# Attention of a two-block model, stepped by single heads or by pairs of heads, on one Trainium2 core

## Chip, core and metric

The program runs on one NeuronCore of a Trainium2 chip. The metric is the device time of one execution in microseconds (us), smaller is better. PE is the matrix engine (TensorE), with PEld its weight loads; DVE is the vector engine, ACT the scalar engine, POOL GpSimd, SP the queue that starts the weight transfers. PSUM is the memory that PE writes, in banks of 128 partitions by 512 float32.

## The reference

Two blocks of a latent/context model, all in float32, with 256 latent and 256 context tokens of width 1024. The first block (gated linear attention, a state-space mixer, their feed-forward parts) and the feed-forward parts and experts of the second are not touched. The two attention mixers of the second block are. The even one has 8 heads of width 64: for latent queries a neighbourhood attention with a table of biases over 256 latent keys, joined in one softmax with 256 context keys; for context queries plain attention over the context. The odd one has, for latent queries only, 8 window heads with a sink, and 4 differential heads.

```python
def joint_softmax(parts, extra=None):
    m = parts[0].max(-1, keepdims=True)
    ...
    return [e / den for e in es]

def neighbourhood_attention(q, k, v, k_ctx, v_ctx, rpb):
    ...
    s_loc = jnp.einsum('bhrqd,bhrjkd->bhrqjk', qg, kg, preferred_element_type=jnp.float32) * scale + bias
    s_ctx = jnp.einsum('bhrqd,bhld->bhrql', qg, k_ctx, preferred_element_type=jnp.float32) * scale
    p_loc, p_ctx = joint_softmax([s_loc.reshape(b, h, rows, GRID_W, kh * GRID_W), s_ctx])
    ...

def diff_attend(q, kvs, lam):
    ...
        a = (p[:, :, 0] - lam * p[:, :, 1]).astype(v.dtype)
        o = jnp.einsum('bhqk,bhkd->bhqd', a, v)
```

## The kernel before

The program is a list of stages (lines 3198 to 3226). Each stage gives a part to PE, ACT and DVE, and the engines meet at a barrier between most stages. Products are numbered in the order in which PE makes them; a product takes the next of eight PSUM banks, PE waits in `B.empty` until that bank's earlier product was freed, and the reader waits in `B.full`.

The stage `Attention` (lines 2439 to 2608) runs twice: once with the items of `even_attention` (32 items: 4 feature tiles f by 4 query tiles t by 2 heads; t 0 and 1 are latent, with 512 keys and a bias, t 2 and 3 context, with 256 keys), once with those of `odd_attention` (16 window items with bias and sink, then 8 differential items of two score maps each). An item is one head and 128 queries. No queue or planner is in play: `for n in range(-ahead, N + 1)` steps through the items, with `ahead` = 2.

- **Scores** (`pair_pe`, L2480 to L2487; L2505 for the differential items). The items of a pair lie in the two halves of the partitions. For a biased pair PE first writes the bias into the bank as a product with the identity matrix (L2480), adds the scores of the 256 latent keys (L2483), then makes those of the context keys (L2487).
- **Maximum** on DVE (L2569), scaled and negated (L2574, or L2571 with the sink); then the **exponential** with its row sum on ACT (L2549). A differential item's two maps are weighed and combined on DVE (L2580 to L2583), in the same step in which their maxima are taken: DVE waits there for ACT.
- **Turned copies**: PE turns the weights 128 by 128 (L2512), ACT copies them to SBUF (L2539).
- **Outputs** (L2519): the turned weights are the stationary side, the values (64 or 128 columns) move. DVE divides by the row sum as it takes them out of PSUM (L2598); for differential items ACT first forms a root (L2556 to L2559).
- **Outputs turned**: every 8 even items (and every pair of query tiles in the odd stage) PE turns the outputs into feature-major order (L2528), and DVE copies them out (L2604, L2606).

```python
                    for it, bank in zip(its, banks):
                        pe.matmul(bank[:, 0:LAT], ident, it["bias"], start=True, stop=False)
```

Of the kernel before, what the change touches and what calls it, by code (L numbers as in the profile page):

```python
# [16 lines left out]
ALU = mybir.AluOpType  # L17
ACT = mybir.ActivationFunctionType
AX = mybir.AxisListType
# [220 lines left out]
def build(nc, I, out, stop=None):  # L240
    ctx = ExitStack()
    with ctx:
# [2053 lines left out]
        m_s = [[uT[:, 2 * i + j, :] for j in range(2)] for i in range(2)]  # L2296
        m_pt = [uT[:, 4 + i, :] for i in range(2)]
# [141 lines left out]
        class Attention(Stage):  # L2439
            all_banks = True  # L2440

            def __init__(self, items, turns, ahead):
                self.items, self.turns, self.ahead = items, turns, ahead
                self.maps = list(itertools.accumulate(len(it["maps"]) for it in items))
                N, order = len(items), []  # L2450
                for n in range(-ahead, N + 2):
                    for m in self.scored(n + ahead):
                        order += [("s", m, j) for j in range(len(items[m]["maps"]))]
                    if 0 <= n < N:
                        order += [("t", n, 0)]
                    if 0 <= n - 1 < N:
                        order += [("o", n - 1, 0)]
                    if n - 2 in turns:
                        order += [("f", n - 2, 0)]
# [3 lines left out]
            def paired(self, n):  # L2463
                first = n - n % 2
                return all(len(it["maps"]) == 1 for it in self.items[first:first + 2])

            def scored(self, n):

                if n >= len(self.items):
                    return []  # L2470
                return [n] if not self.paired(n) else [] if n % 2 else [n, n + 1]

            def pair_pe(self, pe, B, n):

                its = self.items[n:n + 2]
                banks = [B.empty(pe, self.order["s", n + a, 0]) for a in range(2)]
                nk, biased = its[0]["nk"], its[0]["bias"] is not None
                if biased:
                    for it, bank in zip(its, banks):
                        pe.matmul(bank[:, 0:LAT], ident, it["bias"], start=True, stop=False)  # L2480
                    for it, bank in zip(its, banks):
                        q, k = it["maps"][0]
                        pe.matmul(bank[:, 0:LAT], q, k[:, 0:LAT], start=False, stop=True)  # L2483
                at = LAT if biased else 0
                for it, bank in zip(its, banks):
                    q, k = it["maps"][0]
                    pe.matmul(bank[:, at:nk], q, k[:, at:nk], start=True, stop=True).then_inc(B.full_sem, 1)  # L2487

            def score(self, n, j):
                return m_s[n % 2][j][:, 0:self.items[n]["nk"]]  # L2490

            def stats(self, n, j):
                o = 12 * (n % 4) + 6 * j
                return [small[:, o + x:o + x + 1] for x in range(6)]

            def pe(self, pe, B):
                for (kind, n, j), i in self.order.items():
                    it = self.items[n]
                    nk = it["nk"]
                    if kind == "s" and self.paired(n):  # L2500
                        if n % 2 == 0:
                            self.pair_pe(pe, B, n)
# [19 lines left out]
                    else:  # L2522
                        dst, src, gain, made = self.turns[n]
                        for m in made:
                            B.freed(pe, self.order["o", m, 0])
# [839 lines left out]
```

## Time and profile before

| | us |
|---|---|
| median of 3 runs | 2741.61 (2740.02 to 2743.09) |
| the profiled execution | 2740.08 |
| its span, first to last instruction | 2738.2 |
| mean granted TensorE clock | 0.986 of 2.4 GHz |
| even attention stage, first product to last instruction | 1591.66 to 1651.74 |
| odd attention stage | 2238.36 to 2317.17 |

The profile counts an engine as busy while an instruction of its runs. A float32 matmul is two records ("x4" in the chain of waits is two matmuls), a transpose one record. Records of one group overlap, so their mean duration is no pitch; the pieces of the chain give the pitch.

### The profile page before, as it was taken

The page shows a single profiled execution, that of the slowest core. Times are in us where ns is not written, and L with a number is a line of the kernel's source. Part 1 is how long each engine was busy: PE and PEld are TensorE (multiplying, and loading weights), DVE is VectorE, ACT ScalarE, POOL GpSimd, SP SyncE. Part 2 cuts the span into 40 slices and gives each one's busy share as a digit, 9 for nine tenths or more (in the row PEclk, how much of TensorE's full clock was granted, in tenths as well). Part 3 has the DMA queues.
Part 4 walks back from the last instruction along what each step waited for, and adds up shares of the span by engine and source line. Part 5 has one row for each costly group of instructions (what it writes and reads, how often), then busy time and mean ns, then how long its engine had stood idle before and what let it go on. Part 6 is the DMA issues. An engine that isn't in the chain of part 4 may idle for free.

```text
span 2738.2 us, 38420 instructions
## 1 busy us (share of the span) xinstructions
PE 2635.7 (96%) x15510; PEld 1856.4 (68%) x15510; DVE 1402.4 (51%) x2724; ACT 571.8 (21%) x1142; POOL 546.1 (20%) x420
## 2 busy tenths in 40 slices
PE   8999999999989999999999999999999998999998
PEld 4348478888855665789964464888888756655554
DVE  2756376467757778533557542765555335410111
ACT  1216121100043333222022041100000325201110
POOL 0000035444400000047830000444453000000000
PEclk9999999999999999999999999999999998999998
DMA  9540035565242432545445301454543300499995
GB/s 349 196 163 32 31 136 195 176 207 178 88 108 74 112 98 80 162 158 166 154 130 202 137 32 46 170 191 162 163 141 118 119 1 1 166 419 411 415 410 228
DMA packets 222417, 446.71 MB, mean 163 GB/s; under 512 B 18873, under 2 KB 124152, under 8 KB 219162
## 3 DMA queue, kind: packets, MB, share of 16 engines
q1 hardware_dynamic: 180896, 329.78, 33.6%
q10 hardware_dynamic: 41338, 114.40, 12.5%
q8 instruction: 126, 2.06, 0.3%
q14 instruction: 57, 0.47, 0.0%
HBM read 443.01 MB, written 1.13 MB: 162 GB/s over the span
## 4 chain that ended last, share of the span: by engine, by line
PE 91%; DVE 5%; ACT 2%; issue 1%; POOL 0%; DVEq 0%; DMA 0%; ACTq 0%; SPq 0%; POOLq 0%
PE bank L1138 34%; PE bank L966 24%; PE bank L3010 5%; PE bank L990 4%; PE bank L3029 3%; PE bank L982 2%; PE bank_pair L3010 2%; PE bank L559 1%; PE bank L2519 1%; PE bank L3046 1%; PE bank L2095 1%; PE bank_pair L3029 1%; PE bank L2088 1%; PE bank L2512 1%; PE bank L2983 1%
## 5 line engine op out<-in xcount | busy, mean ns | idle before, releaser
L1138 PE MATMUL bank<-arena,slot 128*128 128x256 f32 (+1 forms) x3704 | 677.0, 343 | 6.3 <-DVE arena L1118 2.9
L1138 PEld LDWEIGHTS bank<-arena,slot 128*128 128x128 f32 x3704 | 605.0, 191 | 70.5 <-issue 8.0
L1151 POOL TENSOR_TENSOR slot<-slot 128x512 f32<-128x512 f32 (+3 forms) x208 | 269.8, 1297 | 1566.8 <-PE bank L1138 703.0
L966 PE MATMUL bank<-uT,slot 128*128 128x512 f32 (+2 forms) x1312 | 485.0, 525 | 2.7 <-ACT arena L2128 2.7
L966 PEld LDWEIGHTS bank<-uT,slot 128*128 128x128 f32 (+1 forms) x1312 | 246.7, 190 | 217.0 <-issue 204.8
L1138 PE MATMUL bank<-uT,slot 128*128 128x256 f32 (+1 forms) x1728 | 334.3, 350 | 8.6 <-ACT uT L731 8.4
L1138 PEld LDWEIGHTS bank<-uT,slot 128*128 128x128 f32 x1728 | 290.2, 191 | 46.3 <-ACT uT L731 12.1
L1152 POOL TENSOR_TENSOR slot<-slot 128x512 f32<-128x512 f32 (+3 forms) x208 | 287.2, 1381 | 0.0
L966 PE MATMUL bank<-arena,slot 128*128 128x256 f32 (+1 forms) x576 | 185.0, 484 | 3.8 <-DVE arena L1817 2.3
L966 PEld LDWEIGHTS bank<-arena,slot 128*128 128x128 f32 x576 | 111.9, 195 | 75.6 <-issue 66.7
L700 DVE SCALAR_TENSOR_TENSOR arena<-arena 128x1024 f32<-128x1024 f32 x95 | 122.3, 1297 | 18.8 <-issue 15.0
L990 PE MATMUL bank<-slot,uT 128*128 128x512 f32 (+1 forms) x320 | 120.1, 530 | 0.0
L990 PEld LDWEIGHTS bank<-slot,uT 128*128 128x128 f32 x320 | 55.8, 190 | 61.0 <-issue 60.6
L700 DVE SCALAR_TENSOR_TENSOR arena<-arena,bank_pair 128x1024 f32<-128x1024 f32 x78 | 94.7, 1215 | 2.3 <-issue 1.9
L2210 DVE SCALAR_TENSOR_TENSOR arena<-arena,vectors 128x512 f32<-128x512 f32 (+1 forms) x128 | 87.7, 685 | 4.6
L3010 PE MATMUL bank<-slot,arena 128*32 128x352 f32 x984 | 77.5, 459 | 0.0
L3144 DVE TENSOR_TENSOR arena<-bank_pair,arena 128x352 f32<-128x352 f32 x5 | 2.6, 514 | 140.8 <-PE bank_pair L3010 140.8
L1040 DVE SCALAR_TENSOR_TENSOR hT<-bank,mod,hT 128x256 f32<-128x256 f32 (+1 forms) x48 | 18.9, 435 | 104.1 <-PE bank L966 104.1
L1288 ACT ACTIVATE arena<-arena 128x2048 f32<-128x2048 f32 (+1 forms) x16 | 23.7, 1484 | 230.7 <-DVE arena L1193 173.0
L3144 DVE TENSOR_TENSOR arena<-bank,arena 128x352 f32<-128x352 f32 x16 | 7.9, 495 | 120.2 <-PE bank L3010 120.1
L982 PE MATMUL bank<-uT,slot 128*128 128x512 f32 (+1 forms) x192 | 65.9, 504 | 1.3 <-DVE uT L736 1.3
L3010 PE MATMUL bank<-arena 128*32 128x352 f32 x800 | 63.5, 459 | 0.0
(462 smaller groups left out, 3075.1 us busy)
## 6 DMA issues: line engine op xcount, KB each, us to landing
slot<-in_ffn_w SPq DMA_DIRECT2D x42, 2048.0 KB, 8.8
arena<-in_ada_wt ACTq DMA_DIRECT2D x100, 512.0 KB, 3.6
slot<-in_moe_w SPq DMA_DIRECT2D x62, 704.0 KB, 16.8
arena<-in_moe_w SPq DMA_DIRECT2D x52, 704.0 KB, 17.6
rstd<-in_ada_wt ACTq DMA_DIRECT2D x48, 512.0 KB, 3.5
slot<-in_moe_w SPq DMA_DIRECT2D x11, 2048.0 KB, 18.7
slot<-in_ssd_w_in SPq DMA_DIRECT2D x32, 512.0 KB, 6.9
uT<-in_ada_wt ACTq DMA_DIRECT2D x28, 512.0 KB, 3.6
```

The lines of the kernel that those rows point to most:

```text
L559: ins = pe.matmul(bank[:, :], first_w[:, k, n * P:n * P + P], uT[:, k, :], start=(k == 0), stop=(k == KD - 1))
L700: ins = dve.scalar_tensor_tensor(out=self.room[n % ROOMS] if last else self.spare, in0=self.room[n % ROOMS], scalar=1.0, in1=self.row(blk, ...
L966: ins = pe.matmul(bank[0:m, 0:t1 - t0], w[:, k, c0:c0 + m], x[:, k, t0:t1], start=(k == 0), stop=(k == kt - 1))
L982: ins = pe.matmul(bank[0:m, 0:t], w[:, k, c0:c0 + m], uT[:, k, 0:t], start=(k == 0), stop=(k == KD - 1))
L990: ins = pe.matmul(bank[:, 0:c1 - c0], x[:, k, t * P:t * P + P], w[:, k, c0:c1], start=(k == 0), stop=(k == kt - 1))
L1138: ins = pe.matmul(bank[:, u * n:u * n + n], a[:, k, u * P:u * P + P], x[:, k, :], start=(k == 0), stop=(k == self.h - 1))
L1151: pool.tensor_tensor(out[:, :, 0:c], x[:, :, 0:c], y[:, :, 0:c], op)
L1152: pool.tensor_tensor(out[:, :, c:2 * c], x[:, :, c:2 * c], y[:, :, c:2 * c], op)\
L2088: pe.matmul(o, s_xdt[k % 2][:, h, :], s_m[k % 2][:, h, :], start=True, stop=False)
L2210: ins = dve.scalar_tensor_tensor(out=acc, in0=s_raw[:, j, 0:n, tap:tap + LAT], scalar=vc("conv_w", 32 * tap + f), in1=acc, op0=ALU.mult, o ...
L3010: ins = pe.matmul(bank[32 * g:32 * g + 32, 0:FG], x, w[:, 0, c:c + FG], start=(k == 0), stop=(k == KD - 1))
L3029: ins = pe.matmul(banks[s][32 * c:32 * c + 32, 0:DG], m_turned_hid[:, q, s, :], w[:, q - a, c * DG:c * DG + DG], start=(q == 0), stop=(q = ...
```

## The change

The unit of both attention stages is now a pair: two heads of 128 queries each, or the two maps of a differential head (16 units per stage). In step j PE makes the scores of unit j + 2, turns the weights of unit j, makes the outputs of unit j - 1, and turns outputs of unit j - 3 (differential only).

- The bias product on PE is gone. DVE takes the maximum of the context keys, then one `tensor_tensor_reduce` adds the bias to the latent scores in PSUM and carries the maximum on. Scores are one matmul of up to 512 columns per head.
- The weights are divided by their row sum on DVE before they are turned (`normalise`), a step ahead; the differential combination (`combine`) also moved to the step after its exponentials.
- Outputs are made feature-major: the values are stationary (64 columns), the turned weights move (128 columns), and the two heads go to partitions 0 to 63 and 64 to 127 of one bank. DVE copies 128x128 to the result. The turning of outputs is left for differential heads alone.
- ACT's order in a step is: turned copies of j, root of j - 2, exponentials of j + 2, with one drain per pair where there was one per map.

```diff
-                if biased:
-                    for it, bank in zip(its, banks):
-                        pe.matmul(bank[:, 0:LAT], ident, it["bias"], start=True, stop=False)
-                    ...
+            def scores(self, pe, B, u):
+                it = self.units[u]
+                banks = [B.empty(pe, self.order["s", u, a]) for a in range(2)]
+                for (q, k), bank in zip(it["maps"], banks):
+                    pe.matmul(bank[:, 0:it["nk"]], q, k, start=True, stop=True).then_inc(B.full_sem, 1)
+
+            def turn(self, pe, B, u, a):
+                pe.wait_ge(*S("pn").taken("pe"))
+                bank = B.empty(pe, self.order["t", u, a])
+                for t in range(self.units[u]["nk"] // P):
+                    ins = pe.transpose(bank[:, t * P:t * P + P], self.score(u, a)[:, t * P:t * P + P], ident)
+                ins.then_inc(B.full_sem, 1)
+
+            def outputs(self, pe, B, u):
+                ...
+                        for a, v in enumerate(it["v"]):
+                            ins = pe.matmul(bank[64 * a:64 * a + 64, 0:P], v[t], self.weights(u, a, t), start=(t == 0),
+                                            stop=(t == last))
+                ins.then_inc(B.full_sem, 1)
-                for n in range(-self.ahead, N + 1):
-                    ...
+            def act(self, act, B, ch):
+                for j in self.steps():
+                    if self.has(j):
+                        self.copy_turned(act, B, j)
+                    if self.has(j - 2) and self.units[j - 2]["sub"]:
+                        self.output_root(act, B, ch, j - 2)
+                    if self.has(j + 2):
+                        self.exponentials(act, B, j + 2)
+
+            def maxima(self, dve, ch, B, u):
+                it, (mx, nm) = self.units[u], self.stats(u)[0:2]
+                for a in range(2):
+                    bank, m = B.full(dve, self.order["s", u, a]), mx[:, a:a + 1]
+                    at = 0 if it["bias"] is None else LAT
+                    n = ch(dve.tensor_reduce(m, bank[:, at:it["nk"]], AX.X, ALU.max))
+                    if at:
+                        ch.wait(n)
+                        s = bank[:, 0:at]
+                        n = ch(dve.tensor_tensor_reduce(out=s, in0=s, in1=it["bias"][a], scale=1.0, scalar=m, op0=ALU.add,
+                                                        op1=ALU.max, accum_out=m))
+                ch.wait(n)
+                ...
+
+            def normalise(self, dve, ch, u):
+                it, (den, es, rc) = self.units[u], self.stats(u)[2:5]
+                dve.wait_ge(*S("pr").taken("dve"))
+                ...
+                dve_link(ch, dve.reciprocal(rc, den))
+                for a in range(2):
+                    s = self.score(u, a)
+                    dve.tensor_scalar(s, s, rc[:, a:a + 1], None, ALU.mult).then_inc(*S("pn").given())
+
+            def dve(self, dve, B, ch):
+                for j in self.steps():
+                    if self.has(j + 2):
+                        self.maxima(dve, ch, B, j + 2)
+                    if self.has(j + 1):
+                        if self.units[j + 1]["sub"]:
+                            self.combine(dve, ch, j + 1)
+                        else:
+                            self.normalise(dve, ch, j + 1)
+                    if self.has(j - 1) and not self.units[j - 1]["sub"]:
+                        i = self.order["o", j - 1, 0]
+                        dve.tensor_copy(self.units[j - 1]["o"], B.full(dve, i)[:, 0:P]).then_inc(*B.free(i))
+                    ...
```

PE in the even stage before, one biased pair in the steady part (`bank` and `bank_pair` are PSUM banks, `const` holds the identity, `arena` queries, keys, biases and values, `uT` the weights and their turned copies):

```order
L2480 MATMUL bank<-arena,const 128x256 x2
L2483 MATMUL bank<-arena 128x256 x2
L2487 MATMUL bank<-arena 128x256 x2
L2512 MATMUL bank<-const,uT 128x128 x2
L2519 MATMUL bank_pair<-arena,uT 128x64 x2
L2512 MATMUL bank_pair<-const,uT 128x128 x2
L2519 MATMUL bank<-arena,uT 128x64 x2
```

The same place in the changed kernel, two steps:

```order
L2479 MATMUL bank<-arena 128x512 x2
L2486 MATMUL bank<-const,uT 128x128 x4
L2501 MATMUL bank<-uT,arena 64x128 x8
L2479 MATMUL bank_pair<-arena 128x512 x2
L2486 MATMUL bank<-const,uT 128x128 x4
L2501 MATMUL bank<-uT,arena 64x128 x4
```

The bias products are gone, the scores are one matmul of 512 columns per head, and turning and outputs, which alternated head by head, now follow each other pair by pair; the outputs have 64 output partitions each.

DVE at the same place before, two items:

```order
L2569 TENSOR_REDUCE small<-bank 128x1
L2574 TENSOR_SCALAR small<-small 128x1
L2596 RECIPROCAL small<-small 128x1
L2598 TENSOR_SCALAR arena<-bank_pair,small 128x64
L2569 TENSOR_REDUCE small<-bank 128x1
L2574 TENSOR_SCALAR small<-small 128x1
L2596 RECIPROCAL small<-small 128x1
L2598 TENSOR_SCALAR arena<-bank,small 128x64
```

And in the changed kernel, one step (the `ISA` rows of L2576 are the `tensor_tensor_reduce` and a second instruction of one element for its result):

```order
L2572 TENSOR_REDUCE small<-bank 128x1
L2576 ISA bank,small<-bank,arena,small 128x256
L2576 ISA small 128x1
L2572 TENSOR_REDUCE small<-bank 128x1
L2576 ISA bank,small<-bank,arena,small 128x256
L2576 ISA small 128x1
L2583 TENSOR_SCALAR small<-small 128x2
L2592 RECIPROCAL small<-small 128x2
L2595 TENSOR_SCALAR uT<-uT,small 128x512 x2
L2619 COPY arena<-bank_pair 128x128
```

DVE gains two passes over the latent scores and two over the whole weights per pair, and the division at the outputs has become a copy.

## Rows read from the trace of the kernel before

**Rows 1.** The page, busy time of each engine.

```profile
PE 2635.7 (96%) x15510; PEld 1856.4 (68%) x15510; DVE 1402.4 (51%) x2724; ACT 571.8 (21%) x1142; POOL 546.1 (20%) x420
```

**Rows 2.** Windows: length, busy PE, PEld, DVE, ACT, POOL, clock, DMA, GB/s.

```profile
1590.90:1651.90 61.00, 58.27 (x434) 46.33 (x433) 35.28 (x132) 35.24 (x97) 0.00 (x0) 1.00 0.10 36
2237.60:2317.30 79.70, 66.54 (x433) 49.43 (x433) 49.58 (x160) 47.34 (x137) 0.00 (x0) 0.92 0.00 1
...
2286.00:2288.00 2.00, 0.01 (x1) 0.00 (x0) 0.91 (x6) 1.71 (x5) 0.00 (x0) 1.00 0.00 0
2288.00:2290.00 2.00, 0.53 (x2) 0.29 (x2) 1.90 (x7) 0.00 (x0) 0.00 (x0) 0.50 0.00 0
```

**Rows 3.** Chain of waits, even stage: start us, us, what.

```profile
1612.29 0.45 PE bank_pair L2528 x4
1612.73 0.63 PE bank L2487 x4
...
1618.59 0.92 PE bank L2480 x4
...
1620.14 0.43 PE bank L2487 x4
...
1627.00 0.63 PE bank L2487 x4
```

**Rows 4.** Chain of waits, odd stage.

```profile
2274.37 1.06 PE bank L2505 x4
...
2280.26 0.61 DVE small L2569
...
2284.74 0.61 DVE small L2569
...
2304.98 0.28 ACT arena L2556
...
2306.05 0.21 ACT small L2559
...
2309.78 0.76 DVE uT L2583
...
2316.69 0.48 DVE arena L2606
```

**Rows 5.** Chain of waits in the state-space mixer, matmuls of 64 output partitions.

```profile
824.27 0.37 PE bank L2088 x4
824.64 0.22 PE bank L2090 x4
```

**Rows 6.** Groups by form on DVE: busy us, mean ns of one, idle before.

```profile
L2569 DVE TENSOR_REDUCE small<-bank 128x1 f32<-128x512 f32 x37 | 25.4, 685 | 33.0 <-PE bank L2487 29.9 <-PE bank_pair L2487 2.6 <-PE bank L2505 0.4
L2569 DVE TENSOR_REDUCE small<-bank 128x1 f32<-128x256 f32 x11 | 4.6, 419 | 0.5 <-PE bank_pair L2487 0.3 <-PE bank L2487 0.3
L1040 DVE SCALAR_TENSOR_TENSOR hT<-bank,mod,hT 128x256 f32<-128x256 f32 x32 | 14.7, 479 | 62.6 <-PE bank L966 62.6
L2208 DVE TENSOR_SCALAR arena<-arena,vectors 128x512 f32<-128x512 f32 x24 | 11.5, 479 | 0.3
L2208 DVE TENSOR_SCALAR arena<-arena,vectors 128x256 f32<-128x256 f32 x8 | 2.8, 345 | 0.1
L2574 DVE TENSOR_SCALAR small<-small 128x1 f32<-128x1 f32 x48 | 7.4, 154 | 1.6
L518 DVE COPY vectors<-bank 128x128 f32<-128x128 f32 x4 | 1.1, 288 | 1.2 <-PE bank L513 1.2
```

**Rows 7.** Groups by form on ACT, odd stage.

```profile
L2549 ACT ACTIVATE uT<-bank,small 128x512 f32<-128x512 f32 x22 | 15.0, 681 | 5.3 <-DVE small L2574 4.7
L2539 ACT ACTIVATE uT<-bank 128x512 f32<-128x512 f32 x19 | 11.3, 594 | 11.1 <-PE bank L2512 9.5 <-issue 1.3
L2547 ACT ACTIVATE small<-sinks,small 128x1 f32<-128x1 f32 x16 | 4.6, 286 | 3.6 <-DVE small L2571 3.5
L2549 ACT ACTIVATION_READ_ACCUMULATOR uT<-bank,small 128x1 f32 x22 | 4.3, 196 | 0.0
```

More of the change, by code:

```diff
@@ new lines, in steps, with has, turned, score @@
+            def steps(self):
+                return range(-2, len(self.units) + 3)
+            def has(self, u):
+                return 0 <= u < len(self.units)
+            def turned(self, u):
+                return 1 if self.units[u]["sub"] else 2
+            def score(self, u, a):
+                return uT[:, 2 * (u % 2) + a, 0:self.units[u]["nk"]]
+            def weights(self, u, a, t):
+                return uT[:, 4 + 2 * (u % 2) + a, t * P:t * P + P]
+            def stats(self, u):
+                o = 12 * (u % 4)
+                return [small[:, o + 2 * x:o + 2 * x + 2] for x in range(6)]
@@ new lines, in outputs @@
+            def outputs(self, pe, B, u):
+                it = self.units[u]
+                bank = B.empty(pe, self.order["o", u, 0])
+                for a in range(self.turned(u)):
+                    B.freed(pe, self.order["t", u, a])
+                last = len(it["v"][0]) - 1
+                for t in range(last + 1):
+                    if it["sub"]:
+                        ins = pe.matmul(bank[:, 0:P], self.weights(u, 0, t), it["v"][0][t], start=(t == 0), stop=(t == last))
+                    else:
[3 more added lines that the diff above has]
+                ins.then_inc(B.full_sem, 1)
@@ new lines, in turn_outputs @@
+            def turn_outputs(self, pe, B, u):
+                dst, src, gain, made = self.turns[u]
+                for m in made:
+                    B.freed(pe, self.order["o", m, 0])
+                bank = B.empty(pe, self.order["f", u, 0])
+                for t, x in enumerate(src):
+                    ins = pe.transpose(bank[:, t * P:t * P + P], x, ident)
+                ins.then_inc(B.full_sem, 1)
+            def pe(self, pe, B):
+                for j in self.steps():
+                    if j + 2 < len(self.units):
+                        self.scores(pe, B, j + 2)
+                    if self.has(j):
+                        for a in range(self.turned(j)):
+                            self.turn(pe, B, j, a)
+                    if self.has(j - 1):
+                        self.outputs(pe, B, j - 1)
+                    if j - 3 in self.turns:
+                        self.turn_outputs(pe, B, j - 3)
@@ new lines, in output_root @@
+            def output_root(self, act, B, ch, u):
+                rc, x = self.stats(u)[4:6]
+                bank = B.full(act, self.order["o", u, 0])
+                act.activation(m_turned[:, 0:P], bank[:, 0:P], ACT.Square, accum_out=rc[:, 1:2])
+                ch.wait(ch(act.drain()))
+                ch.wait(ch(act.activation(x[:, 1:2], rc[:, 1:2], ACT.Ln, scale=1.0 / P, bias=x[:, 0:1])))
+                act.activation(x[:, 1:2], x[:, 1:2], ACT.Exp, scale=-0.5).then_inc(*S("root").given())
@@ L2649, in odd_attention @@
                 if t:
[L2650 removed]
+                    turns[len(units) - 1] = (m_y[:, 4 + d, 0:LAT], [rows[:, t, 512 + d * P:512 + d * P + P] for t in range(2)],
                                              sub_gain, [diff[d, t] for t in range(2)])
[L2652 removed]
+            return units, turns
         class OddProject(Stage):
```

256 lines of the change are left out of this document (79 added, 177 removed).

## The prediction

> **What bounds the kernel now.** I read the page first, then the stretches of the two attention stages, then the chain of waits inside them, then groups by form for prices. The page has PE busy 96% of the span, the others at half of it or less [rows 1]; work taken from PE should shorten the time wherever PE is last. Only two stretches can move: the even stage, first product to last instruction 60.1 us (1591.66 to 1651.74), and the odd one, 78.8 us (2238.36 to 2317.17). In the even stage PE is busy 58.3 of 61.0 us with DVE and ACT at 35 each: PE bounds it. In the odd stage it is 66.5 of 79.7 at a mean clock of 0.92 [rows 2]: that stage has two halves. Its window items run like the even stage. From the first differential scores on (2274.37) to the end (2317.17) go 42.8 us, in which the chain runs through DVE and ACT: one item's reduction starts at 2280.26, the next at 2284.74, a period of 4.5 us [rows 4]. There DVE takes maxima, waits for ACT's two exponentials and combines, all in one step, and nothing overlaps. PE starves, and the clock pays: after a stretch in which PE was busy 0.01 of 2 us it was granted 0.50 (1.2 GHz) [rows 2].
>
> In the even stage the period is one feature tile (two biased and two unbiased pairs): 1612.73 to 1627.00, 14.27 us [rows 3].
>
> **The change on PE, per pair.** Removed: the bias product, 0.92 us per biased pair [rows 3], 8 in each stage; the turning of outputs, 0.45 per feature tile [rows 3]. Scores: one pair of 512 columns, 1.06 as the differential form shows [rows 4], 0.63 for the unbiased pair [rows 3]. Turning is the same number of transposes: eight at 0.11 (four took 0.45), plus 0.15 for the first, so 1.03; four give 0.59. Outputs before are 16 records of 64 moving columns per biased pair, each no faster than the load of its 128 columns of weights, the 0.11 of a transpose. After the change they are 16 records of 64 output partitions by 128 columns. The state-space mixer has that very form, alternating the halves of a bank: four records in 0.22, the first four after another form 0.37 [rows 5]. So 16 x 0.055 + 0.15 = 1.03; unbiased 0.59; differential outputs stay at 8 x 0.11. Sums: biased or window pair 3.12, unbiased 1.81, differential 2.6 with a share of its output turning. A feature tile would cost PE 2 x 3.12 + 2 x 1.81 = 9.9 us against 14.27. If PE stayed the bound, that would be all.
>
> A row shows what speaks against it: the same four records of L2487 take 0.63 behind outputs of another form and 0.43 behind scores of their own [rows 3], 0.2 for a change of form; the 0.15 above is the other such change. There are three per pair now, two before. The Trainium skill, TensorEngine Tiling (Array Packing), section Key Properties, says that changing the tiling mode drains the engine. The trace agrees in kind, and its price is already in the sum (0.5 per pair). The cost is hidden as long as PE isn't last.
>
> **The change on DVE, per pair.** This is where the work went. Biased pair: per head a 256-wide reduction from PSUM 0.419 [rows 6], a link of 0.03, and the new `tensor_tensor_reduce` over 256. No row shows it. The nearest is the two-input operation of 256 columns with a PSUM input and a pointer scalar, 0.479 [rows 6]; I take that and 0.02 for the second instruction. From below, 0.42, a plain pass of that width; from above, an addition and a reduction separately, 0.479 + 0.419 = 0.90. Then the negated maximum for both heads 0.154 + 0.03, the reciprocal 0.154 + 0.03, two multiplications in SBUF at 0.479 (0.345 for 256 columns), and the copy 0.288 [rows 6]: 1.90 + 0.18 + 0.18 + 0.96 + 0.29 = 3.51. Unbiased: 0.84 + 0.37 + 0.69 + 0.29 = 2.19. Window pair: 3.51 plus adding the sink 0.18, 3.69. Differential: two reductions of 512 at 0.685 [rows 6], 1.37; negated maxima 0.18; the combination 0.76 [rows 4] and the three small ones ahead of it with their links, some 0.65; scaling some 0.35 (the copy's 0.288 and a pointer scalar); half a turned copy 0.24 (0.48 [rows 4]): 3.55.
>
> The Trainium skill, same page, section PSUM Bottleneck, warns that tiling speeds up TensorE and not the emptying of PSUM. By the sums above that is what happens: DVE's 11.4 per feature tile (2 x 3.51 + 2 x 2.19) beats PE's 9.9.
>
> **On ACT, per pair.** Two exponentials 0.681 + 0.196 and two copies 0.594 [rows 7]: 2.95; window pairs add 2 x 0.286 [rows 7], at most 3.5. Differential: one copy, two exponentials, and the root chain, 1.28 from 2304.98 to the end of the last at 2306.26 [rows 4], less its gap, 1.15: 0.59 + 1.75 + 1.15 + one drain 0.1 = 3.6. It is level with DVE.
>
> **Does the order let DVE run on?** The longest loop is: maxima of unit u, exponentials on ACT (about 1.9), normalisation one DVE step later. Between the maxima of u and its normalisation DVE has the normalisation of u - 1, a copy and the maxima of u + 1: 1.1 + 0.3 + 2.1 = 3.5 biased, 0.9 + 0.3 + 1.0 = 2.2 unbiased. Both cover 1.9. PE makes the scores of j + 2 before it waits for the weights of j, so DVE finds its next banks full. The second turning of a window step takes the bank of the last exponentials but one, freed about when it is wanted. For differential units the combination now comes a full step after the maxima, which is the wait removed. What is late next is DVE itself, and ACT beside it.
>
> **The sum.** Even stage: first scores 1.2 us, 4 x 11.4 = 45.6, tail after DVE's last normalisation (turn, copy, outputs, copy) 2.0, and 1.2 for steps whose longest part changes engine: 50.0, so 10.1 less than 60.1. Odd stage: 1.2, 8 x 3.69 = 29.5, 8 x 3.6 = 28.8, tail; the tail was 2310.54 (end of the combination at 2309.78) to 2317.17, 6.6 us [rows 4], of which 0.6 is in the differential sum and a little falls away, so 5.8; and 1.2: 66.5, 12.3 less than 78.8. Together 22.4. The profiled execution took 2740.08, which gives 2717.7; the median of the runs lies 1.5 above it, so **2719**. Nothing outside waits for anything but the barrier: in the 50 us before the next stage the weight queue stands still with its buffers full (mean DMA share 0.10 [rows 2], all of it at the start), and the experts' transfers start on the router's result, which comes earlier by the same amount.
>
> **Rivals.**
> 1. The new reduction costs as much as two operations. Then 32 of them cost 0.42 more each, on the engine that is last: +13.4, **2732.6**. For: it writes back to PSUM and reads two memories. Against: the two-input row does one pass at 1.04 ns a column. Chance 0.08.
> 2. The clock dips in the differential half. PE will be busy 2.6 of 3.6 us there, and at half clock wants 5.2, 1.6 over the unit; three or four units so, and tails at 1.2 GHz in both stages, give +6 to +9, **2727**. For: the dip after an idle stretch [rows 2]. Against: idle comes in pieces under 1 us now. Chance 0.07.
> 3. It goes the other side: PE, no longer full, is held at 1.2 GHz through both stages. Its full-speed work is 4 x 9.9 + 8 x 3.12 + 8 x 2.6 = 85 us; with a share s at half clock it is 85(1 + s), and with 12 us of ends it passes the present 139 at s = 0.5. At s = 0.8, 165: **2766**. For: PE falls from 96% of the even stage to some 87%, and 72% of the differential half. Against: gaps are short, and a slow PE fills its own gaps, so that the cause goes away. The Trainium skill, TensorE: Matmul & The Clock Gate, section HAM oscillation, describes kernels whose matmul bursts each start cold because of waits between them; by that rule the time would be this rival's. The one dip here followed an empty stretch, which the change removes. Chance 0.03.
> 4. It doesn't do what it says: banks or the order make each engine wait in turn, and the period stays near 14. Then **2739**. The loops above exclude it except for something I haven't seen. Chance 0.03.
>
> **How the numbers follow.** The forecast has the rest, 0.79. Its own range: DVE's small instructions overlap their neighbours by some 0.05 each, ten per pair, which could give 8 us until PE and ACT are reached (2711); steps that alternate between engines could cost 0.5 per step more (+8, 2727). With rival 2 and half of rival 1 the range is 2711 to 2731; rivals 3, 4 and most of 1 are left out, 0.14 at most. Faster than 2736.1 (0.2%, about what this measurement can tell from no change): 0.93. Within 0.2%: 0.03. Slower: 0.04, rival 3 and a hundredth for the unknown.
>
> **What would show it.** Right: even stage near 50 us with DVE busy about nine tenths and PE under that, a feature-tile period of 11 to 12; L2576 near 0.48; four records of L2501 in 0.22; differential units every 3.6 us with chain pieces on both ACT and DVE; clock 1.00 in both steady parts. Wrong: a period over 13, PE waiting in `turn` for ACT rather than DVE, L2576 near 0.9, or a clock under 1 in the even stage.

## The result, and the profile after

| | before | changed |
|---|---|---|
| median of 4 runs, us | 2740.82 (2737.86 to 2743.09) | 2708.78 (2706.22 to 2711.01) |
| ratio | | 0.9883, 95% interval 0.9866 to 0.9901 |
| profiled execution / its span | 2740.08 / 2738.2 | 2708.02 / 2706.2 |
| even stage, first scores to last instruction | 60.1 | 1590.48 to 1638.85 = 48.4 |
| from there to the odd stage's first scores | 586.6 | 588.3 |
| odd stage | 78.8 | 2227.14 to 2285.72 = 58.6 |

The forecast was 22.4 us less; it became 32. The time lies just under the range. The spans differ by 32.0: 11.7 from the even stage, 20.2 from the odd one, 1.7 lost between them, and the rest, 1.7, from the stretches ahead (1.2) and behind (0.6), which vary by more than that between two traces of the changed kernel (1.4 and 2.0).

Busy times of each stage and of pieces of it (windows: length, busy PE, PEld, DVE, ACT, POOL, clock, DMA, GB/s); they answer to [rows 2]:

```profile
1602.87:1613.94 11.07, 10.17 (x89) 6.27 (x90) 9.67 (x37) 8.21 (x24) 0.00 (x0) 1.00 0.00 0
2244.76:2251.50 6.74, 6.47 (x59) 4.11 (x58) 6.39 (x26) 5.80 (x17) 0.00 (x0) 1.00 0.01 2
2267.03:2276.01 8.98, 8.25 (x55) 5.39 (x54) 8.66 (x26) 8.08 (x28) 0.00 (x0) 1.00 0.00 1
1598.00:1600.00 2.00, 2.00 (x10) 1.35 (x9) 1.70 (x7) 1.48 (x6) 0.00 (x0) 0.50 0.03 8
1590.40:1638.90 48.50, 41.70 (x352) 26.23 (x352) 39.11 (x144) 32.94 (x96) 0.00 (x0) 0.96 0.13 45
2227.00:2285.80 58.80, 49.70 (x360) 31.96 (x360) 50.41 (x164) 45.00 (x137) 0.00 (x0) 0.94 0.00 1
```

The first three rows are one feature tile (four pairs), two window pairs, three differential units. No engine is full in a tile; in the two others DVE's 6.39 of 6.74 and 8.66 of 8.98 are as full as its records show. The fourth is a piece of the even stage's start, at 1.2 GHz.

The chain of waits through one feature tile (start us, us, what), in place of [rows 3]; its second half:

```profile
1605.84 0.34 DVE small L2572
...
1607.93 0.50 DVE uT L2595
...
1608.47 1.09 PE bank L2486 x8
1609.57 0.59 PE bank L2501 x8
1610.15 0.63 PE bank L2479 x4
1610.79 1.02 PE bank_pair L2486 x8
1611.81 1.02 PE bank L2501 x16
1612.83 1.11 PE bank L2479 x4
1613.94 0.42 DVE small L2572
```

From 1602.87 to 1608.47 it lies on DVE (the two biased pairs' maxima, divisions and a copy), from there to 1613.94 on PE, which catches up with the transposes, outputs and scores: 5.6 and 5.5 us. The two engines take turns at being last.

A window pair, all of it on DVE:

```profile
2244.76 0.34 DVE small L2572
...
2245.13 0.49 DVE bank L2576
2245.62 0.06 DVE small L2576
2245.68 0.29 DVE small L2572
...
2246.74 0.08 DVE small L2591
...
2247.05 0.88 DVE uT L2595 x2
2247.93 0.20 DVE arena L2619
2248.13 0.34 DVE small L2572
```

And the groups by form of those lines (busy us, mean ns of one, idle before), even stage and, for the last two rows, odd stage:

```profile
L2572 DVE TENSOR_REDUCE small<-bank 128x1 f32<-128x256 f32 x26 | 10.4, 418 | 10.6 <-PE bank L2479 9.1 <-PE bank_pair L2479 1.5
L2576 DVE CUSTOM_DVE_ANT_0 bank<-bank,arena,small 128x256 f32<-128x256 f32 x12 | 5.9, 493 | 0.4
L2576 DVE DVE_READ_ACCUMULATOR2_ANT small<- 128x1 f32 x16 | 2.3, 142 | 0.0
L2595 DVE TENSOR_SCALAR uT<-uT,small 128x512 f32<-128x512 f32 x16 | 7.1, 483 | 0.3
...
L2591 DVE TENSOR_TENSOR small<-small 128x2 f32<-128x2 f32 x8 | 1.2, 155 | 0.0
L2619 DVE COPY arena<-bank 128x128 f32<-128x128 f32 x6 | 1.7, 284 | 0.0
```

Read the two views against each other: a reduction whose record lasts 418 ns moves the chain by 0.34 behind a copy and 0.29 behind L2576; the small L2591 (155 ns) by 0.08, the copy (284 ns) by 0.20, two multiplications of 483 ns by 0.88. Neighbours' records overlap. The window pair takes 3.37, where the sum of means said 3.69.

At the start of the odd stage the chain lies on PE, at the low clock:

```profile
2233.40 1.97 PE bank_pair L2486 x8
2235.37 2.01 PE bank L2479 x4
2237.38 1.81 PE bank L2486 x8
```

These are 5.8 us; the same three pieces take 1.09, 1.06 and 1.02 later in the stage, at 1.00.

One differential unit, in place of [rows 4]; here the chain runs on ACT:

```profile
2270.02 0.60 ACT uT L2534
2270.61 0.29 ACTq L2553
...
2270.97 0.30 ACT small L2554
...
2271.30 0.20 ACT small L2555
2271.51 0.58 ACTq L2546
2272.08 0.76 ACT uT L2544 x3
...
2273.01 0.60 ACT uT L2534
```

2.99 us a unit: turned copy, root chain, then two exponentials, whose part (L2546, L2544) is 1.34, against 1.75 in the forecast. The root chain with its waits (L2553 to L2555) is 0.90, against 1.25 with its drain; the waits between the pieces give 0.15 back.

### The profile page after: what moved, and what is told of

It is laid out like the page before. It is cut to its first block, busy times and chain, and to the rows that moved or that the text cites. A ratio compares the mean times of both kernels' runs of the same rounds, so it can differ in the third digit from the quotient of the medians.

```text
span 2706.2 us, 37981 instructions
## 1 busy us (share of the span) xinstructions
PE 2602.3 (96%) x15358; PEld 1817.8 (67%) x15358; DVE 1407.0 (52%) x2740; ACT 568.7 (21%) x1142; POOL 544.9 (20%) x420
## 3 DMA queue, kind: packets, MB, share of 16 engines
q10 hardware_dynamic: 41338, 114.40, 12.5%
## 4 chain that ended last, share of the span: by engine, by line
PE 88%; DVE 6%; ACT 2%; DMA 1%; issue 1%; POOL 0%; SPq 0%; ACTq 0%; DVEq 0%; POOLq 0%
PE bank L1138 35%; PE bank L966 24%; PE bank L3021 5%; PE bank L990 4%; PE bank L3040 3%; PE bank L982 2%; PE bank_pair L3021 2%; PE bank L559 1%; DMA arena<-in_moe_w 1%; PE bank L2095 1%; PE bank L3057 1%; PE bank_pair L3040 1%; PE bank L2088 1%; PE bank L2994 1%; PE bank L2308 1%
## 5 line engine op out<-in xcount | busy, mean ns | idle before, releaser
L966 PE MATMUL bank<-uT,slot 128*128 128x512 f32 (+2 forms) x1312 | 485.1, 525 | 3.0 <-ACT arena L2128 3.0
L966 PEld LDWEIGHTS bank<-uT,slot 128*128 128x128 f32 (+1 forms) x1312 | 246.8, 190 | 217.3 <-issue 205.0
L966 PE MATMUL bank<-arena,slot 128*128 128x256 f32 (+1 forms) x576 | 184.5, 483 | 3.4 <-DVE arena L1817 2.3
L966 PEld LDWEIGHTS bank<-arena,slot 128*128 128x128 f32 x576 | 111.4, 194 | 75.0 <-issue 66.3
L990 PEld LDWEIGHTS bank<-slot,uT 128*128 128x128 f32 x320 | 55.8, 190 | 61.0 <-issue 60.6
L1040 DVE SCALAR_TENSOR_TENSOR hT<-bank,mod,hT 128x256 f32<-128x256 f32 (+1 forms) x48 | 18.9, 436 | 103.6 <-PE bank L966 103.6
```

The source lines that it names most:

```text
L966: ins = pe.matmul(bank[0:m, 0:t1 - t0], w[:, k, c0:c0 + m], x[:, k, t0:t1], start=(k == 0), stop=(k == kt - 1))
L990: ins = pe.matmul(bank[:, 0:c1 - c0], x[:, k, t * P:t * P + P], w[:, k, c0:c1], start=(k == 0), stop=(k == kt - 1))
```

## The experiments

Single runs of one kernel spread over some 5 us (see the ranges above), so each is judged by the length of its stages in its trace. Two traces of the changed kernel agree there: 48.37 and 58.58 us in the first, 48.35 and 58.57 in a second one. Where the clock fell at a stage's start in one kernel and not in another, the lengths hold that too, and the text says so. The kernel before, run once beside each group, took 2739.33 (first four), 2738.38 (next four) and 2738.36 us (the four after).

### One part undone

**The bias back on PE.** DVE reduces over all columns once.

```diff
+                    for bias, bank in zip(it["bias"], banks):
+                        pe.matmul(bank[:, 0:LAT], ident, bias, start=True, stop=False)
...
-                    at = 0 if it["bias"] is None else LAT
+                    at = 0
```

> The changed kernel with the bias again a product on PE, and one 512-wide reduction per head on DVE. In the changed kernel a feature tile of the even stage takes 11.07 us with PE busy 10.2 of it and the stage 48.4, the odd stage 58.6. Theory 1 (DVE sets the pace and the bias belongs there): DVE gets about 1.0 us per biased pair less, PE 0.92 more, so PE becomes the bound: a tile of about 12.0, even stage about 52, window pairs 4.1 instead of 3.4 and the odd stage about 64, execution about 9 us longer. Theory 2 (moving the bias gave little, the steps are bound by something else that both versions share): under 3 us longer in all.

2715.16 us; even stage 51.5 (1591.01 to 1642.48), odd 60.9. A tile took 12.38 with PE busy 12.02 of it: PE is last again. Undone, the edit costs 3.1 + 2.3, and by the pitches more: a window pair took 4.17, 0.8 above the changed kernel, yet the odd stage missed its 64. PE had less of a pause at both starts and its clock was 1.00 through both stages, where the changed kernel's fell; by the runs with products of constants below, that can be worth up to 1.4 and 1.1 us to this variant.

**Outputs row-major again**, and turned on PE.

```diff
-                            ins = pe.matmul(bank[64 * a:64 * a + 64, 0:P], v[t], self.weights(u, a, t), ...
+                            ins = pe.matmul(bank[:, 64 * a:64 * a + 64], self.weights(u, a, t), v[t], ...
```

> The changed kernel with the outputs again row-major (turned weights stationary, 64 columns of values moving, the two heads side by side in one bank), DVE's copy of 128x128 as it is, and the turning of outputs on PE and its copy on DVE back. Theory 1 (the half-array form runs two at a time, 0.055 us a record): outputs cost PE 1.68 instead of 1.03 per biased pair, 0.84 instead of 0.59 unbiased, and 0.45 plus a copy of 0.69 per tile come back: PE about 12.4 a tile, even stage about 54, odd about 63, 10 us in all. Theory 2 (a change of form costs as much as is won, outputs are hidden): under 3 us in all, of which the copies on DVE are most.

2723.42 us; even 57.4 (1590.38 to 1647.75), odd 62.7: 9.0 and 4.1 more. Its chain of waits has the old form's price:

```profile
1613.23 1.73 PE bank L2502 x16
1614.96 1.06 PE bank L2479 x4
```

1.73 for what takes 1.02 in the new form, and a tile of 13.0. In the even stage this is the largest of the four parts undone here.

**The combination back in the step of its maxima.**

```diff
-                        if self.units[j + 1]["sub"]:
-                            self.combine(dve, ch, j + 1)
...
+                    if self.has(j + 2) and self.units[j + 2]["sub"]:
+                        self.combine(dve, ch, j + 2)
```

> The changed kernel with the combination of the two differential maps taken in the same DVE step as their maxima, as before the change. Theory 1 (the step of delay is what freed the differential half): DVE waits for two exponentials again in each unit, period 4.0 to 4.5 us instead of 2.9 to 3.0, odd stage 8 to 11 us longer, even stage the same. Theory 2 (the half was freed by the order on ACT, the one drain per pair and the fewer bank waits): period under 3.4, odd stage under 4 us longer.

2712.67 us; even 48.4 as it should, odd 71.1 (2222.59 to 2293.73), 12.5 more. (The total shows less, since the even stage began at 1586.01 in this run, 4.5 us earlier than in the changed kernel, and the stretch behind the odd one was 3.3 us shorter: variations outside attention.) The chain has the wait of before:

```profile
2254.29 1.21 DVE small L2572 x2
...
2255.72 0.69 ACT uT L2544
2256.41 0.80 ACTq L2546
...
2257.82 0.75 DVE uT L2605
...
2258.77 1.21 DVE small L2572 x2
```

4.48 us a unit, the 4.5 of before, of which DVE waits some 1.5 for ACT.

**Exponentials ahead of the turned copies on ACT** (with a wait that PE has turned the weights they overwrite, which this order needs).

```diff
+                    if self.has(j) and self.has(j + 2):
+                        B.full(act, self.order["t", j, self.turned(j) - 1])
+                    if self.has(j + 2):
+                        self.exponentials(act, B, j + 2)
                     if self.has(j):
                         self.copy_turned(act, B, j)
```

> The changed kernel with ACT's order turned round: exponentials of unit j + 2 first (after PE has read the weights of unit j, whose place they take), then the turned copies and the root. Theory 1 (with steps this short the order on ACT matters, since PE's outputs wait for the copies and DVE's next normalisation has a whole step): outputs come later, DVE's copy of them and PE's next scores too, 1 to 4 us longer per stage. Theory 2 (ACT has slack of a quarter in the even stage): even stage within 0.5 us, and only the differential half, where ACT is level with DVE, longer.

2724.25 us; even 51.8, odd 69.5: 3.4 and 11.0 more. In the differential half a unit takes 4.97 (2274.97 to 2279.94) and the chain goes exponentials, copy, root, DVE's output, maxima, exponentials: the order on ACT closes a loop that the changed kernel leaves open.

The four cost 5.4, 13.1, 12.5 and 14.4, 45 in all against a gain of 32. They don't add: each alone brings another engine or loop in.

### A suspected cost taken away

**Two columns of the weights divided instead of all** (the outputs are not normalised: this leaves work out).

```diff
-                    s = self.score(u, a)
+                    s = self.score(u, a)[:, 0:2]
```

> The changed kernel in which normalise multiplies only two of each head's columns by the reciprocal; the other columns stay undivided, so that the division of the weights is left out. It asks how far DVE sets the pace: it loses 0.76 us per biased pair and 0.5 per unbiased one. In the changed kernel a feature tile takes 11.07 us, a window pair 3.37. Theory 1 (DVE and PE take turns within a tile, DVE in the half with the biased maxima): a tile falls to 10.2, where PE is full, and a window pair to 3.2, and no more, since PE's own pieces add up to 10.17 and 3.15; even stage 45, odd 57. Theory 2 (DVE alone is the bound): a tile falls by the whole 2.5 us, under 9.

2703.21 us; even 47.4, odd 56.6. DVE's busy time in the even stage falls from 39.1 to 33.9 us, a seventh, and only 1.0 comes off the stage; a tile still takes 10.83 (1602.53 to 1613.36), of which PE is busy 10.4. DVE's load isn't the bound alone there. In the odd stage 2.0 come off, in part because the clock was low there for 3.4 us of the start in place of 6.8.

**The root without its square and logarithm** (work left out on ACT).

```diff
-                act.activation(m_turned[:, 0:P], bank[:, 0:P], ACT.Square, accum_out=rc[:, 1:2])
-                ...
+                act.activation(x[:, 1:2], x[:, 0:1], ACT.Exp, scale=-0.5).then_inc(*S("root").given())
```

> The changed kernel without the square, its sum and the logarithm of the differential outputs on ACT (one exponential of one element stays, so the scaling is left out). ACT loses about 0.75 us per differential unit. Theory 1 (ACT sets the differential period of 2.99, with DVE right under it at 2.90): the period falls to 2.9 and the tail by 0.7, odd stage 1 to 2 us shorter. Theory 2 (ACT alone is the bound): period 2.3 to 2.5, odd stage over 4 us shorter. The even stage stays at 48.4 under both.

2705.99 us; odd 57.1, 1.5 less. A unit takes 2.89 with a chain on DVE without a gap (2265.64, 2268.53, 2271.42). So DVE's pitch there is 2.9, and ACT's 2.99 hides it by a tenth.

**Products of constants where PE would be idle**, ahead of the first turning of a stage and ahead of the last turning of outputs, so that its clock stays up.

```diff
+                    if j == 0:
+                        bank = B.empty(pe, self.order["t", 0, 1])
+                        for _ in range(4):
+                            pe.matmul(bank[:, 0:470], one, const[:, 0:470], start=True, stop=True)
```

> The changed kernel with matmuls of constants into a bank still unused, where PE has nothing to do: four of 470 columns after the third pair of scores in each attention stage, three before the last turning of differential outputs. In the changed kernel PE is granted 0.50 right after that wait, and eight transposes there take 1.9 us instead of 1.0. Theory 1 (the low clock at the stage's start lies on the chain, which runs through PE there): clock 1.00 throughout, even stage 1 to 2 us shorter, odd 3 to 4, and the residual stage behind it loses its 2 us of low clock. Theory 2 (DVE has enough to do meanwhile): under 1 us in all, or longer by what the constants' matmuls overrun the wait.

2705.90 us; even 47.0, 1.4 less; odd 59.0, 0.4 more. The clock was 1.00 in both. The odd stage's 0.4 is the difference of two effects. The window pairs are now a chain on DVE from the start, and the maxima of the fifth begin 13.1 us behind the first scores (2225.52 to 2238.58). The changed kernel needed 14.2 (2227.14 to 2241.30), and its chain went through the slow PE: 1.1 won, and kept up to the last unit. From the last unit's maxima to the end it took 12.1 us, 10.5 in the changed kernel: the products ahead of the tail pushed real ones back, 1.6 lost.

### Order and banks

**Biased and plain pairs alternating** in the even stage, to spread DVE's load.

```diff
-            for f, t in itertools.product(range(4), range(4)):
+            for f, t in itertools.product(range(4), (0, 2, 1, 3)):
```

> The changed kernel with the query tiles of the even stage in the order 0, 2, 1, 3, so that biased and unbiased pairs alternate. In the changed kernel a tile takes 11.07 us with DVE busy 9.67 and PE 10.17: its chain lies on DVE for 5.6 us (the two biased maxima) and on PE for 5.5 (the biased turnings and outputs). Theory 1 (steps whose longest part changes engine cost the difference): with both kinds in each step neither engine waits, a tile takes 10.2 to 10.4, even stage 3 us shorter. Theory 2 (the 11.07 is a loop of dependences between the engines, of the same length in any order): within 0.5 us. The odd stage stays at 58.6.

2716.18 us; even 51.1, 2.8 more. Of this, 1.1 is there by the fifth unit (the clock was low for 6.8 us at this start, in place of 3.4), and 1.6 comes in the steady part. The chain of waits shows why:

```profile
1609.16 0.69 ACT uT L2544
...
1609.94 0.68 ACT uT L2544 x2
...
1610.66 1.09 PE bank_pair L2501 x16
1611.75 0.62 PE bank_pair L2479
```

The outputs are released by an exponential, and the loop scores, maxima, exponentials, outputs closes every two units, in 5.8 us. Outputs need no exponential of that step, only a bank: products take the eight banks in turn, and the outputs' bank is the one that these exponentials read. That reading is inferred; the next runs test it.

**Banks by role** (four for scores, two for turned weights, two for outputs), then the alternating order with it, then that with the outputs' copies on ACT.

```diff
+                    if kind == "s":
+                        roles.append(2 * (u % 2) + a)
+                    elif kind == "t":
+                        roles.append(4 + (u % 2 if self.units[u]["sub"] else a))
```

> The changed kernel with that table of banks and its own order of tiles. Theory 1 (within a tile the chain changes from DVE to PE, no bank is waited for): tile 11.07 as before within 0.1, even stage within 0.5 us of 48.4, odd within 1 of 58.6. Theory 2 (the ring of eight banks costs here too): tile under 10.8.

> The interleaved kernel with another table of PSUM banks in both attention stages: four banks for scores, two for turned weights, two for outputs, in place of the ring of eight, in which the outputs of unit j - 1 take the bank of unit j + 1's second scores, just read by ACT. In the interleaved run two units took 5.79 us and its chain went scores, maxima, exponentials, outputs. Theory 1 (that loop, closed by the bank, was what held it; the engines' own work would fit in 5.1): two units take 5.1 to 5.3 us, a tile 10.2 to 10.6, even stage 45 to 46.5, under the 48.4 of the changed kernel. Theory 2 (the outputs wait for ACT's turned copies in any case, which stand in front of those exponentials or behind them): two units stay at 5.6 or more, even stage over 50.

> All three together: interleaved tiles, the table of banks, copies of outputs on ACT. If inter_roles brings the even stage to 45 to 46.5 and act_copies shortens the odd one by 1 to 1.5, this gives 45 to 46 and 57 to 57.5, an execution 4 us shorter than the changed kernel. The rival is that ACT, in the interleaved even stage, becomes part of the loop and the copies cost there 0.3 per unit: even stage 1 to 4 us above inter_roles.

2716.21, 2713.61 and 2711.67 us. Even stage 49.5, 49.3 and 47.7; odd 60.6, 60.6 and 60.8. With separate banks the exponentials are gone from the even stage's chain in the alternating order, and two units take 5.41 instead of 5.79 (not the 5.1 to 5.3 expected). That bears the reading out: a tile of 10.8, where the changed kernel's takes 11.07. In the changed kernel's own order the banks change nothing in the steady part, 30.3 us from the fifth unit to the last with either table. The whole stages say it less well, because their starts differ: with the table of banks the clock was low for 6.8 us there, and in the last of the three kernels it did not fall at all. So the 0.7 won in the even stage by all three together is less than a full clock at the start was worth above (1.4).

The 2 us that the odd stage loses lie in its tail (12.7 us from the last unit's maxima, in place of 10.5). The chain shows the last unit's weights waiting for the bank of the turned outputs, since in this table both use the same two:

```profile
2283.25 0.40 DVE arena L2647
...
2283.79 0.64 PE bank L2505 x4
```

**The outputs' copies on ACT**, one unit later, in the changed kernel's order and banks.

```diff
+                    elif self.has(j - 2):
+                        i = self.order["o", j - 2, 0]
+                        act.activation(self.units[j - 2]["o"], B.full(act, i)[:, 0:P], ACT.Copy).then_inc(*B.free(i))
```

> The changed kernel with the copies of outputs on ACT, between the turned copies and the exponentials, instead of on DVE. Theory 1 (window pairs are a gapless chain of DVE instructions, in which the copy stands for 0.20 us): a window pair takes 3.2 instead of 3.37, odd stage 1 to 1.5 us shorter; in the even stage the copy lies in the chain twice a tile, 1 us shorter at most. Theory 2 (ACT then comes to its exponentials later, 0.29 per pair, and DVE waits for them): window pairs 3.4 or more.

2705.99 us; even 48.3, the same; odd 58.1, 0.5 less (1 to 1.5 expected). A window pair takes 3.17, as expected; of the 0.8 that four of them win, 0.6 is left at the last unit and 0.5 at the end.

### Both ends together, and the changed kernel again

Products of constants (two of 380 columns at the tail, a step later) and the outputs' copies on ACT.

> The changed kernel once more, timed in the same rounds as the next one. Theory (the stages are now bounded by DVE's and ACT's pitches and by low clock at two starts): 2706 to 2709 us, even stage 48.4, odd stage 58.6. Rival (the shares of before and after shown so far are a drift of the chip): over 2712 or below 2703.

> Products of constants ahead of the first turning of each stage and ahead of the last turning of the odd one, and the outputs' copies (unit j-2) moved from DVE to ACT. Theory that the ends are separate and add: even stage 47.0 (low clock at its start gone), odd stage 57.6 (window pairs 3.1 instead of 3.37, tail as before), residual stage behind at full clock, 1.7 less: about 4 us less than the changed kernel in the same rounds. Rival that ACT's queue ends the window pairs as soon as DVE's is shorter: odd stage 58.6, and 2 us less in all. Rival that the products of constants push the real ones back: even stage over 48.4, no gain.

The changed kernel: 2707.88 us (2704.84 to 2711.33), ratio to before 0.9878, interval 0.9863 to 0.9893. The other: **2699.56 us** (2695.76 to 2702.73), 0.9851, 0.9837 to 0.9864; it is the shortest of all here, 8.3 us under the changed kernel in the medians, twice what was expected. Their traces, in us:

| | even | between | odd | behind |
|---|---|---|---|---|
| changed kernel again | 48.35 | 588.3 | 58.6 | 422.5 |
| both ends | 46.97 | 586.6 | 56.75 | 416.4 |

The ends add up, 1.4 and 1.8. The window pairs fell from 3.37 to 3.17 (2246.12 to 2249.29), now a chain on PE alone; by the last unit the odd stage is 2.0 ahead, of which the copies alone gave 0.6 and the full clock at the start the rest. The residual work behind the odd stage (L966), no longer at the low clock (0.54 and 0.60 from 2288 to 2292 in the changed kernel), took 1.7 less (29.57 against 27.88 for the same 128 records). That can't be put down to the products of constants: the four kernels with the old combination, without division, without the root and with only the copies moved have none and took 27.88 there too. With 1.7 from the stretch between and 2.3 from a wait in the last stage (both in the last section) the named pieces make 8.9. The medians differ by 8.3 and these two traces by 11.3; 2.0 of the trace's difference lie behind the odd stage and are not explained (that stretch takes 416.4 to 424.3 us over all the traces).

## Why the prediction was right and wrong

- **PE's prices held.** Sixteen records of L2501 take 1.02 (1.03 forecast from [rows 5]), eight transposes 1.02 to 1.09 (1.03), one pair of scores 1.06 to 1.11 (1.06); PE is busy 10.17 per tile, 9.9 forecast. What a change of form costs was not measured by itself; it is in those figures.
- **The new reduction** is a single pass: L2576 takes 493 ns, 479 forecast. Rival 1 is out. Its second instruction moves the chain by 0.06 to 0.07, 0.02 forecast. (The 1.04 ns a column in rival 1 is the step between the two reductions in [rows 6], 685 and 419 ns, and no figure of L1040's row.)
- **The step that failed is the pricing of DVE and ACT** by sums of mean durations. "DVE's small instructions overlap their neighbours by some 0.05 each" was put in the range and not in the sum; and it isn't only the small ones. Mis-sized by it: 8 differential units, 3.6 forecast, 2.99 measured, 4.9 us; 8 window pairs, 3.69 and 3.37, 2.6 us; 4 tiles, 11.4 and 11.07, 1.3 us. That is 8.8 of the 9.5 us by which the two stages (107.0) beat the forecast (116.5). The tile's 11.07 came near by luck: by the union of its records DVE is busy 9.67 per tile, where the sum said 11.4, and the turn-taking of DVE and PE, which the forecast had at 1.2 us for the whole stage, put 0.9 per tile on top of PE's 10.17. The starts and tails came near by luck too (4.1 and 7.7 us, 4.4 and 8.2 forecast): they hold 1.4 and 1.1 us of low clock, which the sum had at nothing. The Trainium skill, Perfetto Trace Analysis, section DVE / Act Engine Instruction, says that a record of these engines runs on until the write is acknowledged, while the next instruction may begin to read as soon as the one before has executed; the overlaps above agree, and by that rule means should never have been added.
- The biggest miss is ACT in the differential half. The means were read from [rows 7] and added as 0.681 + 0.196 per exponential; but the next exponential starts while the sum of the last is read, so that two move the chain by 1.34 and not 1.75. The root chain, read from one place in [rows 4], was too long by some 0.35: its square (L2552) starts before the copy's record has ended.
- **That DVE bounds the feature tile** was half right. DVE is last for the biased half of a tile, PE for the other (5.6 and 5.5 us). Taking nearly all of the division's columns away gained 1.0 in the whole stage, and the alternating order, which should have spread DVE's load, met the ring of banks.
- **The loops.** "DVE finds its next banks full" held in the window half behind its start. "For differential units the combination now comes a full step after the maxima, which is the wait removed": shown by its undoing, 12.5 us where the whole change gave the odd stage 20.2. The order on ACT, which the prediction took as given, is as necessary: 11.0 us with it undone.
- **The clock.** Rivals 2 and 3 are out: 1.00 in both steady parts. The Trainium skill's rule on bursts that each start cold (TensorE: Matmul & The Clock Gate, section HAM oscillation) has no case here: PE pauses in every step and the clock stays. It fell to 0.50 at both starts, after PE had been idle for 3.5 us in the even stage and 3.4 in the odd one (ahead of the first L2486) while DVE and ACT made the first pair ready. Rival 2 looked for the low clock in the differential half and in the tails, which ran at 1.00; it came at the starts. It cost 1.4 us in the even stage and 1.1 in the odd one, by the kernel with products of constants. That such a pause is always followed by the low clock is not shown: it was not in the odd stage with row-major outputs (3.4 us) nor in the even one with alternating order, banks by role and copies on ACT (3.5 us).
- **"Nothing outside waits for anything but the barrier"** held for the waits and not for the clock, which was lower in the stretch between the stages and took 1.7 back in the traces; whether the change is the cause stays open (last section).

## What to carry to other kernels

Price an engine's step by pitches, the starts of two like instructions in a chain without a gap, and not by adding mean durations: here the sum of means was 9% too long for a row of DVE passes and 20% for ACT's. A pitch is what the chain of waits shows. Then look for a loop between engines before believing in any bound: moving one operation by one step was worth 12 us in the odd stage, and taking a seventh of DVE's work away 1 us in the even one. Undoing the parts one at a time gave shares that add up to more than the whole. And compare pieces of a stage before whole stages: 0.4 us in a total hid 1.1 won at the start and 1.6 lost in the tail.

## What was not expected of the hardware

The stretch between the stages has a pause of PE of some 2.4 us, 70 us behind the even stage, while DVE makes two long passes. The pause is in every trace. In the changed kernel the clock falls behind it, in the kernel before it doesn't. Windows of the changed kernel (second trace) and, below, of the one with both ends at the same place:

```profile
1708.00:1710.00 2.00, 0.28 (x2) 0.00 (x0) 2.00 (x2) 0.00 (x0) 1.48 (x2) 1.00 0.00 0
1710.00:1712.00 2.00, 1.28 (x4) 1.09 (x5) 1.71 (x4) 0.60 (x1) 0.00 (x0) 0.83 0.38 139
1712.00:1714.00 2.00, 2.00 (x6) 1.61 (x5) 1.97 (x2) 0.60 (x1) 0.00 (x0) 0.50 0.94 301
```

```profile
1706.00:1708.00 2.00, 0.48 (x2) 0.08 (x1) 2.00 (x2) 0.00 (x0) 1.68 (x2) 1.00 0.00 0
1708.00:1710.00 2.00, 1.09 (x5) 0.98 (x6) 1.75 (x3) 0.60 (x1) 0.00 (x0) 1.00 0.34 78
1710.00:1712.00 2.00, 2.00 (x11) 1.77 (x10) 1.93 (x3) 0.60 (x1) 0.58 (x1) 1.00 1.01 264
```

The stretch is 586.6 us in the kernel before and in the two with products of constants, and the clock is 1.00 in all of it there. It is 588.2 to 590.0 in the other thirteen traces, all of which have 3.4 us at the low clock behind this pause, and the four at 590 as much again elsewhere in the stretch. So a pause of the same length costs 1.7 us or nothing. A low clock in the even stage ahead of it is not what decides: two of the thirteen (the bias on PE; order, banks and copies together) ran that stage at 1.00. What does decide stays open.

The second is the wait in the last stage, on DVE between the end of its last L3166 and the stored outputs. The chain of waits, changed kernel again and, below, both ends:

```profile
2699.03 2.78 issue
```

```profile
2690.07 0.52 issue
```

It is 2.8 to 3.1 us in thirteen traces, the kernel before among them, and 0.52 in exactly the three whose copies were moved from DVE to ACT (2716 instructions on DVE in place of 2740). Nothing of these instructions is near that stage. The page lists a DMA queue for instructions (q14) with 56 or 57 packets for the changed kernel and 55 with the copies moved, which would fit a piece of DVE's program fetched late; but with the bias on PE it has 55 too, and still fewer instructions on DVE (2676), and the wait was 3.1. So the association is shown and its cause is not. For small differences it means that some 2 us can come from a place far from the edit, and only the trace tells.
